# Expert rows handled one by one: gates on ScalarE, seven ring slots, tables of four steps, and a later timetable for the next front

## The reference

```
q = (xb @ w_query).reshape(PEER_BLOCK, PEER_HEADS, 2, D_SUBKEY)
s = einsum('nhpd,pkd->nhpk', q, sub_keys)
top_s, top_i = lax.top_k(s, TOPK)                      # 16 of 128, for each half
best_s, best_j = lax.top_k(cand_s, TOPK)               # 16 of the 256 pair sums
experts = take_along_axis(cand_e, best_j, axis=-1)     # of 16384
gates = softmax(best_s)
act = gelu(einsum('nd,nhkd->nhk', xb, expert_down[experts]))
out = einsum('nhk,nhkd->nd', gates * act, expert_up[experts])
```

## Time and profile before

| | us |
|---|---|
| median of 3 runs | 2618.66 (2613.66 to 2625.57) |
| the profiled execution | 2613.67, of it 2611.9 span |

### The profile page before, as it was taken

The page is one execution under the profiler, slowest core; times in us unless marked ns, Lnnn a source line. Parts: engine busy times, 40 slices in busy tenths (PEclk is TensorE's granted clock), DMA queues, the critical chain, the costliest instruction groups (busy, mean ns, idle before and its releaser), DMA issues.

```text
span 2611.9 us, 22104 instructions
## 1 busy us (share of the span) xinstructions
PE 1741.7 (67%) x7010; PEld 1228.0 (47%) x7010; DVE 1667.7 (64%) x3646; ACT 572.1 (22%) x1387; POOL 796.7 (31%) x647
## 2 busy tenths in 40 slices
PE   6988838666847877676692854565554077777676
PEld 3758736533636766553381843564453032222121
DVE  1001377778677227777866777877878866766764
ACT  1021111156112002114502101222011132333221
POOL 0000033334323002334433323333333444444442
PEclk9999958977868988787855577777776599999989
DMA  6877799988968349998897889699798899999997
GB/s 210 306 246 252 261 371 360 356 306 297 374 249 353 137 140 338 351 362 308 315 378 273 343 328 354 262 355 351 278 371 314 310 389 412 412 420 404 366 376 294
DMA packets 129305, 841.10 MB, mean 322 GB/s; under 512 B 15487, under 2 KB 20863, under 8 KB 33882
## 3 DMA queue, kind: packets, MB, share of 16 engines
q0 software_dynamic: 86512, 615.29, 61.1%
q1 hardware_dynamic: 37348, 217.83, 23.0%
q10 hardware_dynamic: 5328, 6.56, 0.7%
HBM read 824.39 MB, written 15.22 MB: 321 GB/s over the span
## 4 chain that ended last, share of the span: by engine, by line
DMA 43%; DVE 21%; PE 20%; POOL 6%; issue 5%; ACT 3%; DVEq 2%; ACTq 0%; SPq 0%; POOLq 0%
DMA gather_ring<-in_experts,expert_numbers 41%; DVE gather_ring L1576 7%; PE bank L748 6%; DVE expert_sums L1595 6%; POOL gather_ring L671 6%; PE bank L1002 4%; PE bank L739 4%; PE bank L762 3%; DVEq L1586 1%; DMA expert_sums<-in_g_norm 1%; ACT expert_sums L1253 0%; DVE best_values L1501 0%; DVE scratch_row L1337 0%; ACT expert_coefs L1243 0%; DVE top_values L1501 0%
## 5 line engine op out<-in xcount | busy, mean ns | idle before, releaser
L671 POOL DMA_INDIRECT gather_ring<-in_experts,expert_numbers x576 | 762.9, 1325 | 1769.9 <-DVE expert_sums L1595 891.5
L1576 DVE CUSTOM_DVE_ANT_0 gather_ring<-gather_ring,h_kept 128x1024 f32<-128x1024 f32 x384 | 465.6, 1221 | 292.2 <-DMA gather_ring<-in_experts,expert_numbers 291.7
L1002 PE MATMUL bank<-gather_ring,expert_sums 128*128 128x512 f32 (+1 forms) x768 | 374.4, 635 | 218.6 <-ACT expert_sums L1253 218.4
L748 PE MATMUL bank<-hT,weight_chunks 128*128 128x128 f32 (+2 forms) x2304 | 442.5, 357 | 105.0 <-ACT sigmoids L1163 41.7
L1595 DVE SCALAR_TENSOR_TENSOR expert_sums<-gather_ring,expert_coefs,expert_sums 128x1024 f32<-128x1024 f32 x378 | 468.7, 1281 | 14.5 <-issue 0.4
L748 PEld LDWEIGHTS bank<-hT,weight_chunks 128*128 128x128 f32 x2304 | 405.0, 213 | 138.0 <-issue 36.3
L1232 ACT ACTIVATE expert_acts<-expert_dots 128x2 f32<-128x2 f32 x288 | 58.6, 203 | 1527.1 <-DVE expert_dots L1576 1526.9
L1002 PEld LDWEIGHTS bank<-gather_ring,expert_sums 128*128 128x128 f32 (+1 forms) x768 | 132.1, 181 | 460.3 <-issue 243.6
L1576 DVE CUSTOM_DVE_ANT_0 gather_ring<-gather_ring,u_and_gv 128x1024 f32<-128x1024 f32 x192 | 234.1, 1222 | 164.1 <-DMA gather_ring<-in_experts,expert_numbers 163.9
L739 PE MATMUL bank<-weight_chunks,hT 128*128 128x256 f32 (+1 forms) x960 | 238.2, 409 | 59.9 <-ACT u_and_gv L1066 17.9
L739 PEld LDWEIGHTS bank<-weight_chunks,hT 128*128 128x128 f32 (+1 forms) x960 | 183.4, 195 | 112.0 <-issue 75.5
(11 more groups left out here) (207 smaller groups left out, 1774.0 us busy)
## 6 DMA issues: line engine op xcount, KB each, us to landing
weight_chunks<-in_w_in SPq DMA_DIRECT2D x84, 1024.0 KB, 7.5
weight_chunks<-in_w_ada SPq DMA_DIRECT2D x24, 1024.0 KB, 4.9
weight_chunks<-in_w_query SPq DMA_DIRECT2D x24, 1024.0 KB, 6.8
weight_chunks<-in_w_branch_a SPq DMA_DIRECT2D x12, 1024.0 KB, 6.3
weight_chunks<-in_w_branch_b SPq DMA_DIRECT2D x12, 1024.0 KB, 4.9
weight_chunks<-in_w_out SPq DMA_DIRECT2D x12, 1024.0 KB, 5.0
gather_ring<-in_experts,expert_numbers POOLq DMA_INDIRECT x576, 8.5
u_and_gv<-in_cache_k SPq DMA_DIRECT2D x16, 512.0 KB, 8.5
```

The costliest lines, as they stand in the source:

```text
L671: pool.indirect_dma_start(out=ring[:, item % RING, :], out_offset=None, in_=experts, in_offset=bass.IndirectOffsetOnAxis(ap=expert[:, t, k ...
L748: mm = nc.tensor.matmul(out[:, 0:N], w[:, k, j * P:(j + 1) * P], src[:, k, 0:N], start=(k == 0), stop=(k == KC - 1))
L1002: mm = nc.tensor.matmul(bank[b + half][0:n, :], by[:, r % KEPT, :], up[:, half * 512:(half + 1) * 512], start=(k == 0), stop=(k == TOPK * ...
L1576: nc.vector.tensor_tensor_reduce(out=down, in0=down, in1=h2_of(t), scale=1.0, scalar=0.0, op0=ALU.mult, op1=ALU.add, accum_out=dots[:, c:c ...
```

## The change

Six edits, made together:

1. VectorE handles single rows: `dot(k)`, then the add of row k-1 (`add_row`), instead of pairs.
2. ScalarE multiplies by the gates in the stretches too (`coefficient`): a GELU and a product for each row. VectorE's product and its drain are gone, and the add waits for ScalarE's product.
3. The ring has 7 slots. Expert numbers and gates keep four steps instead of all, which makes the room.
4. Pieces of a front are placed after each row, by `ROW_US = [4.0, 3.0]` per row in place of 5.6 and 5.9 per two rows. The 128 rows of the first stretch then place 512 units (358 before), the 256 of the second 768 (755 before).
5. The six parts of `choose` lie at the rows 1, 3, 5, 7, 9, 12 of a step.
6. In the timetable the gate stands behind the first two results of the merge.

```diff
-RING = 6
-BATCH = 2
+RING = 7
+CHOSEN = 4
-BATCH_US = [5.6, 5.9]
+ROW_US = [4.0, 3.0]
...
-            def gelu(t, k):
+            def coefficient(t, k):
+                n, s = row_number(t, k), seq(t, k // TOPK)
+                c = slice(n % KEPT, n % KEPT + 1)
+                act.wait_ge(s_dot, n + 1)
+                nc.scalar.activation(acts[:, c], dots[:, c], ACT.Gelu).then_inc(s_act, 1)
+                if k % TOPK == 0:
+                    act.wait_ge(s_gates, s + 1)
+                act.wait_ge(s_act, n + 1)
+                nc.scalar.activation(coef[:, c], acts[:, c], ACT.Copy,
+                                     scale=gates[:, s % CHOSEN, k % TOPK:k % TOPK + 1]).then_inc(s_scaled, 1)
...
+                            rows += 1
+                            until(pieces, due, STRETCH_AT[g] + rows * ROW_US[g])
...
-            CHOOSE_AT = (0, 1, 2, 3, 4, 6)
+            CHOOSE_AT = (1, 3, 5, 7, 9, 12)
...
-            def add_rows(t, k):
+            def add_row(t, k):
                 n = row_number(t, k)
-                dve.wait_ge(s_act, n // BATCH + 1)
-                nc.vector.tensor_tensor(coef[:, c], acts[:, c], gates[:, t, k:k + BATCH], ALU.mult)
-                dve.drain()
+                up = ring[:, row_item(t, k) % RING, D:2 * D]
+                a = acc[:, n % 2, :]
+                dve.wait_ge(s_scaled, n + 1)
+                if k < 2:
+                    nc.vector.tensor_scalar(a, up, coef[:, c:c + 1], None, ALU.mult).then_inc(s_vsum, 1)
+                else:
+                    dve.wait_ge(s_vsum, n - 1)
+                    nc.vector.scalar_tensor_tensor(out=a, in0=up, scalar=coef[:, c:c + 1], in1=a, op0=ALU.mult,
+                                                   op1=ALU.add).then_inc(s_vsum, 1)
...
-                            for j in range(BATCH):
-                                dot(t, k + j)
-                            next(ending, None)
+                            dot(t, k)
+                            if r in (0, 2):
+                                next(ending, None)
...
-                            if k:
-                                add_rows(t, k - BATCH)
+                            if k:
+                                add_row(t, k - 1)
```

More of the change, by code:

```diff
@@ L192, in clock @@
             at["pages", g, 1] = now
-        for phase, count, each in (("u", 8, 3.9), ("gv", 4 * n, 3.9), ("gate", 2 * n, 4.0), ("merge", 32, 3.9),
-                                   ("out", 4 * n, 3.9), ("norm2", 2 * n, 4.0), ("query", 16, 4.3)):
-            for j in range(count):
+        for phase, count, each in (("u", range(8), 3.9), ("gv", range(4 * n), 3.9), ("merge", range(2), 3.9),
+                                   ("gate", range(2 * n), 4.0), ("merge", range(2, 32), 3.9), ("out", range(4 * n), 3.9),
+                                   ("norm2", range(2 * n), 4.0), ("query", range(16), 4.3)):
+            for j in count:
                 now += each
@@ L1271, in _ @@
                     due[0] = next(pieces)
-                batch = 0
+                rows = 0
                 for order, t in enumerate(tiles):
@@ L1292, in _ @@
                 for h in range(STEPS[t]):
-                    for r in range(TOPK // BATCH):
-                        diagonals(t, h * TOPK + r * BATCH)
-                        if r == 4 and seq(t, h + 1) < len(CHOICES):
+                    for k in range(TOPK):
+                        diagonal(t, h * TOPK + k)
+                        if k == 9 and seq(t, h + 1) < len(CHOICES):
                             exponentials(seq(t, h + 1))
-                        if order and h == 0 and r == 5:
+                        if order and h == 0 and k == 10:
                             store_y(LATER[order - 1], acc[:, 0, :])
@@ L1640, in _ @@
                 due = [next(pieces)]
-                batch, ending = 0, iter(())
+                rows, ending = 0, iter(())
                 for order, t in enumerate(tiles):
@@ L1675, in _ @@
                     choosing = choose(seq(t, h + 1)) if seq(t, h + 1) < len(CHOICES) else iter(())
-                    for r in range(TOPK // BATCH):
-                        for j in range(BATCH):
-                            dot(t, h * TOPK + r * BATCH + j)
+                    for r in range(TOPK):
+                        dot(t, h * TOPK + r)
                         if r in CHOOSE_AT:
                             next(choosing, None)
-                        if order and h == 0 and r == 3:
+                        if order and h == 0 and r == 6:
                             for _ in finish_later(LATER[order - 1]):
```

75 lines of the change are left out of this document (25 added, 50 removed).

## The result

The changed kernel takes **2344.61 us** (median of four runs, 2341.77 to 2347.14) against 2616.16 (four runs, 2603.43 to 2625.57) for the kernel before on the same chip: ratio 0.8965, interval 0.8923 to 0.9006. A second set of five rounds gave 2341.87 against 2615.17, ratio 0.8945 [0.8918, 0.8972]. The forecast was 2450 with a range of 2375 to 2560.

What follows compares the result with a forecast made beforehand. The prediction took the DMA engines as the floor of both stretches and a chain as the gap's bound. From 2613.67, -93 - 69 - 6 = -168 gave 2446, with a 5 us offset 2450 us; range 2375 to 2560.

Steps and rivals of the forecast that it cites:

- The gap: Between the stretches: 143 us shrinks to about 20; with the first stretch at 547, tile 1's gathers start 93 us earlier.
- the DMA floor: Full work of the DMA engines: 503 us in the first stretch, 957 in the second; taken as the floor of each.
- three floors: First stretch: DMA 503 us, VectorE 430, the front's own pace 474; the highest was taken.
- The shares: Busy share of the DMA engines by which full work was divided: 0.92 in the first stretch, 0.94 in the second.
- the VectorE floor: VectorE's own work: 875 us in the second stretch, 430 in the first.
- The slots and the single rows: Second stretch: 12.5 us of cover against 8.1 to 10.4 removes most of the 192.4 us gather wait, -69 us.
- The new wait for ScalarE: VectorE waits for ScalarE's product behind attention pieces, up to 5 us, ten and eight times: 50 and 40 us per stretch.
- Counted at nothing: The new wait for ScalarE costs nothing beyond the shares of 0.92 and 0.94; 90 us if VectorE were the bound.
- The last stage: Only its ends can gain: 531 to 525 us, -6 us, bounds 0 and -17.
- Full engines: Rival: five gathers under way keep the DMA engines at 0.98 in every stage, -254 us, 2365; chance 0.14.
- Only the gap: Rival: the stretches keep DMA shares of 0.87 and 0.88, only -62 us from the gap, 2557; chance 0.13.
- The front sets the pace: Rival, first stretch: 510 units at 1.44 us each take 736 us, +96 us, 2715; chance 0.06.

Runs made afterwards that it cites:

- timetable alone: The kernel before, in pairs with six slots, with only a later timetable, BATCH_US = [8.0, 6.0] instead of [5.6, 5.9]: 2534.65 us, ratio 0.9675.
- rows alone: The changed kernel with front pieces placed as far apart as before, ROW_US = [2.8, 2.95] instead of [4.0, 3.0]: 2427.22 us, ratio 0.9255.
- piece split: The changed kernel with one more point where ScalarE returns to rows, between the halves of the sample tile's page attention: 2327.4 us, ratio 0.8873; repeated, 2327.84.
- attention spread: The piece split kernel with 4 more timetable units per attention piece and ROW_US = [4.4, 3.2] instead of [4.0, 3.0]: 2347.89 us, ratio 0.8948.

## Why the prediction was wrong

**The gap: right.** 20 us forecast, 19 measured (the tail of tile 0, 9, and choosing, 10). Stretch and gap together came down from 660 to 530 us, by 130 in place of the 93 forecast; by the timetable alone to 580, by 80. The difference is the step below.

**The step that failed: the DMA floor.** The prediction took "0.88 x 1087 = 957 us of full work" and "503 us" as the highest of three floors and divided them by a share. The shares came true. The amounts did not: after the change the same bytes took 0.93 x 965 = 897 us of busy time in the second stretch, and in the first, gap and all, 0.93 x 511 + 0.55 x 19 = 486 where 511 were counted. Busy time is no fixed amount of work: 957 / 0.94 was 53 us too long, and 897 / 0.94 = 954 would have been 11 too short. The row that said so stood in the earlier trace rows: 421 GB/s at share 1.01 in the last stage, beside 394 at 1.00 in a mixed window. The prediction used that row for the last stage only and gave no reason for the difference. The mixed windows at 420 after the change, and the gathers alone at 393 with five slots, show that the mixture alone doesn't make it. In bytes the floor is 330 x 1087 / 421 = 852 us for the second stretch, and (331 x 517 + 148 x 143 - 174 x 19) / 421 = 449 for the first. (The Trainium skill, "HBM Reference", Specifications, gives about 425 GB/s for a core that streams alone. The fullest windows here, 420 to 423, agree with it.) But the forecast's shares over these byte floors would give 449 / 0.92 = 488 and 852 / 0.94 = 906, too little by 23 and 59 us: a floor put right in bytes does not give the time by itself.

**What the second stretch is made of: VectorE's own work and its two waits.** Take from the second stretch of each kernel what VectorE waits there for gathers and for ScalarE's GELU or product, and what is left moves little while VectorE's instructions are the same:

| kernel | second stretch | for gathers | for ScalarE | rest |
|---|---|---|---|---|
| before | 1087 | 192 | 14 | 881 |
| timetable alone | 1079 | 190 | 12 | 877 |
| pairs, seven slots | 1004 | 102 | 25 | 878 |
| the same and timetable | 989 | 98 | 18 | 873 |
| single rows, five slots | 1021 | 116 | 47 | 858 |
| single rows, six | 984 | 83 | 48 | 853 |
| after (seven) | 965 | 66 | 47 | 852 |
| rows alone (seven) | 962 | 70 | 45 | 847 |
| after, piece split | 950 | 66 | 32 | 852 |
| the same, attention spread | 945 | 62 | 26 | 857 |
| after, product on VectorE | 978 | 33 | 37 | 908 |

The rest is 873 to 881 in pairs and 847 to 858 in the single rows that need no products on VectorE (1087 - 192 - 19 for them gave the prediction's 875, with the 14 left in). It is the VectorE floor that the prediction had at 875 and passed over, since the DMA floor of 957 was higher. It was right to 3%, as was the one of the first stretch: 511 - 24 - 49 = 438 against 430. So the forecast of 1018 meant 143 us of waits beside that floor; 113 came, and the floor came 23 lower.

This is an account of VectorE's time and not a bound, as the last row shows. With the product back on VectorE the rest is 56 us longer than after (81 in both stretches, close to the 85 that were worked out), the two waits are 43 us shorter, and the stretch is 13 longer; in the first stretch the rest grew by 25 us and the stretch by 2. So VectorE's own work is not paid in full while there are waits that it can fill. The byte floor and VectorE's rest now lie at about one height, 852 and 852 us in the second stretch and 449 and 438 in the first, and both stretches lie above both. Which of the two a stretch follows, no run parts; in the first one TensorE's front could also hold it, since it took 511 us in three kernels (after, piece split, and pairs with seven slots and the timetable) whose VectorE rests were 438, 438 and 450.

**The slots and the single rows: right in kind, too small.** The 12.5 us of cover against 8.1 to 10.4 took the waits for gathers down as said. The forecast worked that cover out from both edits at once, and the rows show that either does most of it: in pairs the seventh slot took the wait from 190 to 98 (later timetable), single rows at six slots took it from 190 to 83, and both together leave 66. The expectations count the gathers under way as two to four in pairs with six slots and three to five with seven, and as three, four and five in single rows with five, six and seven slots. By the lower count the wait falls in order: 190, then 98 to 116, 83, 66. Which of the edits that came with single rows does it was not parted, but the product's place is not it: with the product on VectorE the wait is 33.

**The new wait for ScalarE: the size came right partly by luck, the price not.** 50 and 40 us were worked out, 48.8 and 47.4 came, but made up otherwise. In place of ten waits of up to 5 us the first stretch has 25 of 2 us in the mean, and half of the 47.4 is one wait, 24 us behind cumulative sums, which was not in the reckoning, since that knew attention pieces only. The 26 more table loads came as counted (203 in the trace) and were not tried by themselves; ScalarE still waits 155.5 us for dots in the first stretch. "Counted at nothing" failed at that one wait: splitting the piece took 15 us of it and the stretch was 15 shorter, so it was paid in full. For the other waits no run shows that: with attention spread, the wait for the product in the first stretch grew by 29 us, and the wait for gathers fell by 19 beside it.

**The last stage: -20 against -6**, just outside the bound of -17. The share rose to 0.97, which gives 504 / 0.97 = 520. The other 9 us were not traced: the bytes per busy time hardly differ (383 / 0.95 = 403 GB/s and 394 / 0.97 = 406), and 2 MB fewer fell into the window. The seventh slot gives most of this gain alone: in pairs the stage takes 513 us with it.

**The rivals.** "Full engines" named 2365 and comes nearest, but that is luck: its shares of 0.98 did not come, they stayed at 0.93. "Only the gap" is what the old rows do with the new timetable. "The front sets the pace" did not happen: 510 units in 511 us, 1.00 us each, where 1.25 would have lost.

**What stays open** is why a busy DMA engine moves more bytes in one window than in another. By gathers alone five slots moved less than seven (391 to 407 GB/s against 412 to 421 at a full share); six in single rows, with 409 to 422, hardly did. With mixed traffic the slots do not show so plainly: with five of them three of the ten full windows ran at 421 or 422 GB/s all the same. And near its end the last stage with seven slots has a window with a share of 1.02 and a low rate, into which small loads for the end of the sample tile fall:

```profile
2210.00:2250.00 40.00, 29.09 (x56) 7.28 (x56) 22.06 (x53) 14.01 (x44) 18.93 (x20) 0.91 1.02 371
```

No row shows inside a packet what the engine waits for.

## What to carry to other kernels

The busy time of the DMA engines isn't a fixed amount of work: work out a floor in bytes, by the best rate that any stage of the trace reaches, and see whether the waits for transfers fit it. Then write the time of a stretch as the own work of the engine that uses the data plus its waits; what was left without the waits stayed within 1% over six variants in single rows, and over the four in pairs. But don't take the parts for a bound: work that was added to VectorE went mostly into its waits. When a wait for data goes, look for the longest wait that is left and try it: here 15 us of it came back in full. And when two edits serve one end, such as more slots and earlier release of a slot, try each without the other in both orders before giving each its share.

## What the runs showed of the hardware

At a busy share of 0.99 to 1.02 the DMA engines moved 391 to 407 GB/s in the last stage with five slots, and 412 to 421 with seven, by gathers alone and of the same form (the eight windows of the five-slot kernel from 1930 to 2250; the six of the kernel after from 1930 to 2170). Near the end of the kernel after, one window with a share of 1.02, with small loads among the gathers, moved only 371. With mixed traffic the full windows rose from 382 and 395 (the only two at 0.99 or more of the kernel before, between 334 and 1934) to 420 to 423 in eleven of the 17 of the kernel after. With pairs, seven slots and the old timetable they lie between, from 372 to 420. In single rows with five slots they run from 385 to 422.
